# A conformer-pooling-SwiGLU block on eight cores: from four token tiles with a bf16 weight scratch to all 2048 tokens resident

## The reference

```python
u = rms_norm(h, g_mix); z = u @ w_in                      # (T, 5 x 1024)
gates = sigmoid(z[3072:] + b_gate)
a = z[:1024] * sigmoid(z[1024:2048])
a = depthwise_conv31(a) + b_dw
y_conv = silu(layer_norm(a, ln_g, ln_b)) @ w_conv_out
m = window_mean(z[2048:3072], (2, 4, 8, 16)) - z[2048:3072]   # 256 channels per window
y_pool = ((m @ w_pool) * pool_scale) @ w_pool_out             # w_pool: 4 blocks of 256 x 256
h = h + (gates[:1024] * y_conv + gates[1024:] * y_pool) @ w_o
v = rms_norm(h, g_ffn)
h = h + (silu(v @ w_ffn_gate) * (v @ w_ffn_up)) @ w_ffn_down  # 2816 wide
out = rms_norm(h, g_final)
```

## Time and profile before

| | |
|---|---|
| median of 3 runs | 1390.31 us (1389.91 to 1393.74) |
| span of the profiled execution, slowest core | 1385.0 us |
| spans of the 8 cores | 1373.7 to 1385.0 us |
| mean granted clock of PE, slowest core | 0.927 |
| busy: PE, DVE, ACT, POOL | 1115.2, 370.9, 339.1, 164.3 us |
| DMA | 229.35 MB, mean 166 GB/s |

### The profile page before, as it was taken

How to read it: one execution, slowest core, us unless ns; L and a number is a source line. 1 busy time by engine, 2 the same in 40 slices (tenths; PEclk the granted TensorE clock), 3 DMA queues, 4 the chain that set the end, 5 groups by cost and what they waited for, 6 DMA issues and landing times.

```text
span 1385.0 us, 16637 instructions; the slowest of 8 cores (1373.7 to 1385.0 us)
## 1 busy us (share of the span) xinstructions
PE 1115.2 (81%) x5862; PEld 505.4 (36%) x5960; DVE 370.9 (27%) x569; ACT 339.1 (24%) x519; POOL 164.3 (12%) x201
## 2 busy tenths in 40 slices
PE   0167587956656799879899998797999998898996
PEld 0033233332222344334444443244444443335443
DVE  0110432221111031532331314513221316323212
ACT  1112252122110023341331122522320234313111
POOL 6050202201000012011000102011000120110001
PEclk9988878987877899989999999899999999899999
DMA  9999999999999876525544457237424664253241
GB/s 165 185 211 192 221 159 168 184 177 173 173 171 157 194 240 150 174 96 170 190 153 168 155 176 208 91 122 246 165 108 173 217 196 139 104 188 148 97 162 61
DMA packets 85773, 229.35 MB, mean 166 GB/s; under 512 B 8351, under 2 KB 60191, under 8 KB 68925
## 3 DMA queue, kind: packets, MB, share of 16 engines
q1 hardware_dynamic: 42512, 166.30, 38.1%
q0 software_dynamic: 38528, 45.09, 24.5%
q10 hardware_dynamic: 4653, 16.90, 3.7%
HBM read 234.69 MB, written 45.09 MB: 202 GB/s over the span
## 4 chain that ended last, share of the span: by engine, by line
PE 46%; another core or an unknown queue 20%; DMA 11%; SPq 11%; DVE 5%; issue 4%; ACT 2%; POOL 1%; DVEq 0%; ACTq 0%; POOLq 0%
PE ps L431 43%; SPq L174 11%; DMA rep_59<-aT 3%; DMA wsc<-w_in 3%; PE ps L552 2%; DMA xres_100<-xe 2%; DMA xres_101<-xe 1%; DMA rep_58<-aT 1%; DVE rstd_ln L673 1%; DVE ub_62 L449 1%; DVE tn_80 L684 1%; PE ps L459 1%; DMA wslot_43<-wsc 0%; ACT sqj L437 0%
## 5 line engine op out<-in xcount | busy, mean ns | idle before, releaser
L441 POOL TENSOR_TENSOR stats<-stats,nhalf_s 128x1 f32<-128x1 f32 (+1 forms) x49 | 27.1, 554 | 634.0 <-DVE stats L439 634.0
L431 PE MATMUL ps<-vT,wslot_45 128*128 128x512 bf16 (+1 forms) x252 | 57.8, 375 | 33.5 <-DMA wslot_45<-wsc 13.2
L431 PE MATMUL ps<-vT,wslot_47 128*128 128x512 bf16 (+1 forms) x283 | 64.8, 373 | 16.9 <-DMA wslot_47<-wsc 10.5
L439 DVE TENSOR_SCALAR stats<-stats 128x1 f32<-128x1 f32 (+1 forms) x49 | 7.5, 153 | 201.3 <-ACT sqj L437 201.3
L431 PE MATMUL ps<-vT,wslot_46 128*128 128x512 bf16 (+1 forms) x267 | 58.0, 360 | 2.0 <-ACT vT L463 1.3
L431 PE MATMUL ps<-vT,wslot_43 128*128 128x512 bf16 x220 | 54.1, 386 | 6.4 <-DMA wslot_43<-wsc 5.4
L459 PE MATMUL ps<-ident_s,ub_61 128*128 128x128 bf16 (+1 forms) x136 | 10.9, 227 | 59.2 <-DVE ub_61 L449 34.6
L431 PE MATMUL ps<-vT,wslot_48 128*128 128x512 bf16 (+1 forms) x250 | 56.4, 365 | 0.9 <-ACT uT_49 L463 0.6
L431 PE MATMUL ps<-vT,wslot_44 128*128 128x512 bf16 (+1 forms) x236 | 54.9, 376 | 1.5 <-ACT vT L463 1.3
L836 DVE TENSOR_TENSOR fT<-ps,sgf_106 128x512 bf16<-128x512 f32 x44 | 30.4, 690 | 90.3 <-PE ps L431 84.4
L747 POOL TENSOR_TENSOR mergedT<-t_0_93,t_0_94 128x512 bf16<-128x512 f32 x16 | 20.2, 1264 | 287.5 <-DVE t_0_93 L744 287.5
(11 more groups left out here) (226 smaller groups left out, 1861.5 us busy)
## 6 DMA issues: line engine op xcount, KB each, us to landing
wslot_44<-wsc SPq DMA_DIRECT2D x22, 1024.0 KB, 9.3
wslot_47<-wsc SPq DMA_DIRECT2D x22, 1024.0 KB, 9.0
wslot_43<-wsc SPq DMA_DIRECT2D x21, 1024.0 KB, 10.6
wslot_45<-wsc SPq DMA_DIRECT2D x21, 1024.0 KB, 7.2
wslot_46<-wsc SPq DMA_DIRECT2D x21, 1024.0 KB, 8.2
wslot_48<-wsc SPq DMA_DIRECT2D x21, 1024.0 KB, 9.7
wsc<-w_in POOLq DMA_DIRECT2D x10, 1024.0 KB, 47.1
rep_58<-aT SPq DMA_DIRECT2D x96, 67.5 KB, 2.8
```

The costliest lines, as they stand in the source:

```text
L431: S.op(PE, lambda e: e.matmul(out, lhsT=lhsT, rhs=rhs, start=start, stop=stop), [lhsT, rhs], [out], signal=signal)
L441: S.op(POOL, lambda e: e.tensor_tensor(out=rs, in0=ms, in1=nhalf[0:n, 0:1], op=ALU.pow), [ms, nhalf[0:n, 0:1]], [rs])
```

## The change

The loop over tiles goes: all 2048 tokens of a core stay on chip, channel-major, and each step of the block runs over all of them.

- **Layout.** The host hands over x, the output and the weights already cut into channel-major blocks. x comes as 5 pieces of 416 tokens, halo included (`xp`), and once more as 4 blocks of 512 (`xr`) for the residual. PE transposes nothing. The RMS norm sums squares over channels: ACT squares, DVE adds the 8 channel groups, one fp32 matmul against ones (1/1024) adds the partitions, and ACT makes exp(-0.5 ln(.)).
- **Weights.** The scratch goes. POOL's DMA reads a chunk of 512 KiB in fp32 and casts it on the way into one of 9 slots, once per kernel (`load_one`); 108 such chunks and 8 of the FFN's down weights (1.4 MiB read each), which have places of their own. `w_pool` comes in fp32, uncast.
- **Order.** `pool_tile` for all pieces; then for each channel group `vg(c)`, `conv(c-1)`, `im2col(c)`; then LayerNorm statistics, fold, gates and projections, output projection, FFN, down projection in four blocks, the last in two halves.
- **im2col.** `a_out` writes a channel group to DRAM (`a_d`) in two parts, and eight DMAs read shifted copies back to `rep`.
- **LayerNorm statistics.** DVE adds d and its square over the channel groups (`acc_s`, `acc_q`); 8 fp32 matmuls instead of 64.
- **Pool map.** `w_pool` x `pool_scale` x `w_pool_out` is multiplied on chip to `weff` (32 matmuls of 512 columns), and the map's own matmuls per token go.
- **Background work.** Window sums and LayerNorm steps lie in a queue `bg` from which `pump(n)` emits n pieces between other instructions on DVE.
- **Spill.** After the output projection h1 is written to DRAM (`h1_d`) and read back for the last addition.

```diff
-        S.dma(SP, slot_sem[s], wslot[s][:, 0:nel], wsc.ap()[n][:, 0:nel], xr=[DRAM_G0 + n])
...
-            dsta = aT[:, :, 0:2 * HALO]
-            S.op(POOL, lambda e: e.tensor_copy(out=dsta, in_=acarry[:, :, 0:2 * HALO]), [acarry[:, :, 0:2 * HALO]], [dsta])
...
-        def im2col(pr):
-            for j in range(4):
-                for s_ in range(4):
-                    ws = 540 if s_ < 3 else 539
-                    o = repS[st][32 * s_:32 * s_ + 32, j, :, 0:ws]
-                    i_ = aT[32 * j:32 * j + 32, 2 * pr:2 * pr + 2, s_:s_ + ws]
-                    S.dma(SP, rep_sem[st], o, i_, val=tot)
...
-    for i in range(NT):
-        tile_body(i)
...
+NSLOT = 9
...
+    def load_one():
+        name, src, raw = wl[wnext[0]]
+        wnext[0] += 1
+        s = free.popleft()
+        whome[name] = s
+        dst = slotf[s][:] if raw else slot[s][:]
+        S.dma(POOL, slot_sem[s], dst, src)
...
+    x_load(0)
+    for _ in range(2):
+        load_one()
+    S.wait_prod(POOL, x_sem[0])
+    prefetch()
+    S.wait_prod(SP, slot_sem[3])
+    x_load(1)
+    S.wait_prod(SP, slot_sem[7])
+    x_load(2)
+    x_load(3)
...
+    def s1_rstd(p):
+        mm(psum[6][:, 0:PW], ones[:], sq0[p % 2][:, 0, :], True, True)
+        act(lnt[:, 0:PW], psum[6][:, 0:PW], AF.Ln, bias=e_rms)
+        act(psum[7][:, 0:PW], lnt[:, 0:PW], AF.Exp, scale=-0.5)
...
+    s1_squares(0)
+    s1_rstd(0)
+    s1_scale(0)
+    for p in range(NPC):
+        if p + 1 < NPC:
+            s1_squares(p + 1)
+        for c in range(KC):
+            pool_tile(p, c)
+            if c == 2 and p + 1 < NPC:
+                s1_rstd(p + 1)
+                s1_scale(p + 1)
+            if p == NPC - 1:
+                release(f"pool{c}")
+        if p == 0:
+            x_load(4)
...
+            while step < wd:
+                nw = width - step
+                dst = (s1, s2)[tgl][:, 0:nw]
+                out.append(lambda dst=dst, a=src[:, 0:nw], b=src[:, step:step + nw]:
+                           tt(DVE, dst, a, b, ALU.add))
+                src, width = dst, nw
+                step *= 2
+                tgl ^= 1
...
+    def vg(c):
+        for p in range(NPC):
+            sl = slice(p * PW, (p + 1) * PW)
+            bv, bg_ = nb(), nb()
+            for k in range(KC):
+                mm(bg_[:, 0:PW], w(f"gate{c}", k), uT[:, k, sl], k == 0, k == KC - 1)
+            for k in range(KC):
+                mm(bv[:, 0:PW], w(f"val{c}", k), uT[:, k, sl], k == 0, k == KC - 1)
+            s_ = sg[p % 2][:]
+            act(s_, bg_[:, 0:PW], AF.Sigmoid)
+            tt(DVE, aT[c % 2][:, sl], bv[:, 0:PW], s_, ALU.mult)
+            if p == 2:
+                a_out(c, 0, 3 * PW)
+            pump(2)
+        a_out(c, 3 * PW, EXT)
+        release(f"gate{c}", f"val{c}")
+    def a_out(c, lo, hi):
+        h = 0 if lo == 0 else 1
+        S.dma(SP, ad_sem[h], a_d.ap()[c][:, lo:hi], aT[c % 2][:, lo:hi], xw=[("ad", c, h)])
+    def im2col(c):
+        for h in range(2):
+            S.wait_prod(SP, ad_sem[h])
+            tot = rep_sem[h].count + 16 * 4
+            for s_ in range(4):
+                src = a_d.ap()[c].rearrange("(j i) t -> i j t", j=4)[:, :, HW_ * h + s_:HW_ * h + s_ + RW]
+                S.dma(SP, rep_sem[h], rep[h][32 * s_:32 * s_ + 32, :, 0:RW], src, val=tot)
+    def conv(c):
+        pump_until(win_done, c)
+        for b in range(NB):
+            h = b // 2
+            ps = nb()
...
+            if c == 1:
+                tt(DVE, acc_s[:, tok], d_sb[0][b][:], d_sb[1][b][:], ALU.add)
+            elif c > 1:
+                tt(DVE, acc_s[:, tok], acc_s[:, tok], d_sb[c][b][:], ALU.add)
+            if c > 0:
+                tt(DVE, acc_q[:, tok], acc_q[:, tok], dq, ALU.add)
+            pump(1)
+        if c + 2 < KC:
+            build_cw(c + 2)
...
+    vg(0)
+    im2col(0)
+    for c in range(1, KC):
+        vg(c)
+        conv(c - 1)
+        im2col(c)
...
+    def A(c, b):
+        ps = tile_mm(f"gA{c}", u_rhs(b))
+        i = sA[c, b] = ztile()
+        act(zt[i][:], ps[:], AF.Sigmoid, bias=pcc(PC_BGA, c))
...
+    def Bm(c, b):
+        ps = tile_mm(f"gB{c}", u_rhs(b))
+        i = t2[c, b] = ztile()
+        act(zt[i][:], ps[:], AF.Sigmoid, bias=pcc(PC_BGB, c))
+    def P(c, b):
+        ps = tile_mm(None, lambda k: mT[:, k, b * TT:(b + 1) * TT], weff_c=c)
+        i = t2[c, b]
+        tt(DVE, zt[i][:], ps[:], zt[i][:], ALU.mult)
...
+    def C(c, b):
+        pump_until(ln_done, b)
+        ps = tile_mm(f"co{c}", lambda k: actT[k][b][:])
+        i, j = sA.pop((c, b)), t2.pop((c, b))
+        tt(DVE, zt[i][:], ps[:], zt[i][:], ALU.mult)
+        tt(DVE, mrg[c][b][:], zt[i][:], zt[j][:], ALU.add)
...
+        mm(pm[:], ones[:], acc_s[:, tok], True, True)
+        mm(pq[:], ones[:], acc_q[:, tok], True, True)
+        i = ztile()
+        act(zt[i][:], pm[:], AF.Square)
+        if b == NB - 1:
+            mean, rstd = pm, psum[7]
+            ids = (i,)
+        else:
+            m_ = ztile()
+            act(zt[m_][:], pm[:], AF.Copy)
+            mean, rstd = zt[m_], zt[i]
+            ids = (i, m_)
+        tt(DVE, zt[i][:], pq[:], zt[i][:], ALU.subtract)
+        act(zt[i][:], zt[i][:], AF.Ln, bias=e_ln)
+        act(rstd[:], zt[i][:], AF.Exp, scale=-0.5)
+        lnm[b] = (mean, rstd, ids)
...
+                d = d_sb[c][b][:]
+                tt(DVE, d, d, mean[:], ALU.subtract)
+                tt(DVE, d, d, rstd[:], ALU.mult)
...
+            ts(DVE, wps[:, g, km, :], src, pcc(PC_PSC, 2 * g + km), ALU.mult)
+        for ki in range(2):
+            for h in range(2):
+                ps = nb()
+                for km in range(2):
+                    mm(ps[:], wps[:, g, km, ki * 128:(ki + 1) * 128],
+                       w(f"po{2 * g + km}", None, h * 512, (h + 1) * 512), km == 0, km == 1)
+                act(weff[:, 2 * g + ki, h * 512:(h + 1) * 512], ps[:], AF.Copy)
+            pump(1)
+        release(f"wpl{g}", f"po{2 * g}", f"po{2 * g + 1}")
...
+    for c in range(1, KC):
+        for b in range(NB):
+            A(c, b)
+            pump(1)
+            Bm(c, b)
+            pump(1)
+            P(c, b)
+            pump(1)
+        release(f"gA{c}", f"gB{c}")
+        for b in range(NB):
+            C(c - 1, b)
+        release(f"co{c - 1}")
...
+    def v_norm(b):
+        h = h1b[b % 3]
+        for c in range(KC):
+            stt(DVE, vT[:, c, b * TT:(b + 1) * TT], h[:, c, :], pcc(PC_GFFN, c), psum[7][:],
+                ALU.mult, ALU.mult)
+        S.dma(SP, sp_sem[b], h1_d.ap()[b], h[:].rearrange("p k t -> p (k t)"))
...
+    for j in range(2, NFC):
+        for b in range(NB):
+            gu(j, b)
+        release(f"fg{j}", f"fu{j}")
+        if j < 2 + KC:
+            c = j - 2
+            S.dma(POOL, fd_sem[c], wfd[c][:].rearrange("p j m -> p (j m)"), w_fd.ap()[c])
...
+    parts = [(0, 0, TT), (1, 0, TT), (2, 0, TT), (3, 0, 256), (3, 256, 256)]
+    for n, (b, o, w_) in enumerate(parts):
+        for c in range(KC):
+            ps = nb()
+            for j in range(NFC):
+                mm(ps[:, 0:w_], wfd[c][:, j, :], fT[j][:, b * TT + o:b * TT + o + w_], j == 0, j == NFC - 1)
```

1119 lines of the change are left out of this document (453 added, 666 removed).

## The result

The changed kernel took 1093.85 us in the median of its five runs beside 1390.31 for the kernel before, 296 us less. It was forecast at 1078, so the forecast was 1.4% short. Executions in which some cores ran at a lower granted clock than the rest (in one of these five 0.84 to 0.86 on one die, and 1231 us) are left out of the ratios and of the times in the experiments. The ratio is 0.785 (95% interval 0.781 to 0.789), from a median of 1091.39 us.

What follows compares the result with a forecast made beforehand. PE was taken as the bound: 985 us of its work plus 32, 5, 16, 12, 5, 6 and 11.5 of idle time and half clock made a 1072.5 us span, 1078 with 5.3 around it; range 1045 to 1165.

Steps and rivals of the forecast that it cites:

- idle in the value/gate loop: Value/gate loop: DVE, at 21.0 us a channel, nearly the bound for six channels; PE idle 5 us (0 to 15).
- start, up to the value/gate loop: Kernel start and pool phase: first matmul at 24 us, another wait of some 8; 32 us idle (24 to 45).
- LayerNorm and fold, idle: Between value/gate loop and gates: PE waits for ACT's four chains and the fold's scaling, 16 us (9 to 22).
- C(0, 3), idle: First convolution projection of block 3: its last 8 normalization steps come late on DVE, 12 us (5 to 14).
- seams of output projection and FFN: PE's idle time at the seams of the output projection and FFN, 5 us.
- the term for half clock: Whole kernel: PE at its lower clock level after four waits, 1.8 us each, 6 us.
- DMA: DMA keeps ahead of PE: 15.3 us a value/gate channel against PE's 21.4, trip covered, cost zero; share under 0.8.
- The first rival: Value/gate loop: a_d and rep move at 108 GB/s, 29.8 us a channel; time 1146; DMA-bound chance 0.21.
- The lower clock: All eight cores granted clock 0.80 under dense matmuls, adding 246 us: 1324; chance 0.08.
- Slower by weight latency: Value/gate, gates and FFN: weight chunks land too late; whole gain lost from 85 us, near 1880 at 126.7; chance 0.05.
- Ln and Exp: LayerNorm chains on ACT: if both share one table set, one load serves both and the sum is 7 us lower.
- Around the span: Time outside the slowest core's span, 5.3 us as in the kernel before, added at the end.

Runs made afterwards that it cites:

- The two experiments on the start: Changed kernel with ScalarE's squares issued a piece sooner, 1078.74 us; and, separately, with token piece 1 loaded right behind piece 0, 1083.17 us.
- the combined kernel: Changed kernel with squares sooner, piece 1 sooner, scalings spread, two LayerNorm steps a tile, weight scaling first, later Ln/Exp, fold copies shared with VectorE: 1057.82 us, ratio 0.755.

## Why the prediction was right, and where it was short

The mechanism held: the span is PE's work plus a few holes. Its terms, against core 3 of the changed kernel:

| term | predicted | measured |
|---|---|---|
| value/gate channel, PE | 21.4 | 21.2 |
| FFN and down with their sums, behind the first tile | 456.9 | 459.1 |
| idle in the value/gate loop | 5 | 1.1 |
| start, up to the value/gate loop | 90 | 112.1 |
| LayerNorm and fold, idle | 16 | 14.4 |
| C(0, 3), idle | 12 | 8.6 |
| seams of output projection and FFN | 5 | 12.5 |
| tail | 11.5 | 10.1 |

(456.9 is 304.1 less the first 16 matmuls, 152.4 and the fp32 sums, four of 0.86 and one of half the width; LayerNorm and fold 289.94 to 318.12 less 13.8 of matmuls; C(0, 3) is PE's waits for SiLU tiles; the seams are 73.8 less 61.3 of matmuls; the tail is 1079.7 to 1089.8.)

Taken together the idle terms came out (32 + 5 + 16 + 12 + 5 + 11.5 = 81.5 us priced, 80.0 measured), but by luck: the start and the seams were too short, the value/gate loop, the fold and C(0, 3) too long. The 17 us that are missing from the span are in the term for half clock. PE was busy for 1009.8 us where I had 985 and 6; summed from PE's timeline, the tiles behind its waits took some 22 us longer than the same tiles at full clock.

- **The start** is the step that failed, and with it the term for half clock. I priced the first matmul at 24 us (27.3) and one more wait of some 8 (6.55), and then let PE run: the prediction named a pool phase that ends far from 90 us as the sign of a mis-sized start, and it ended at 112.1. The missing 22 us are 3.3 at the first matmul, three waits of 2.64 that I had no term for, some 10 at half clock behind all these (my 6 us of half clock were for the whole kernel), and 3.1 of the pieces' sums, which I had counted with PE's work, less 1.5 at the wait for piece 1. What I overlooked is that ACT's squares of piece p+2 stand behind the last copy of piece p. The two experiments on the start take 12.6 and 8.1 us of it, together 18.
- **The seams** were priced at 5 without looking at what stands ahead of the additions on DVE. Spreading the scalings takes 11 of the 12.5 us.
- **DMA.** A value/gate channel was priced at 15.3 us; the share of 0.72 in the middle channels is 15.3 of 21.2. The sum is right, its parts are not: the cast landed 160 GB/s instead of 108, so the trip through DRAM took more than its 10.5. It stays covered, though the share was not under 0.8 everywhere (0.92 and 0.86 in the windows from 125 to 175 us); without cover it costs 15 us a channel. The first rival's time, near 1146, is passed when every im2col is read twice (1190), part of it by DMA time and part by the order in the queue.
- **The lower clock** did not come in the profiled run: 0.98 to 1.00 in every window in which PE is busy throughout, 0.973 to 0.978 over the spans of the eight cores. The Trainium skill (TensorE: Matmul & The Clock Gate, "Seeing it yourself") would have 13/16 under dense matmuls of several cores of a die; the profiled run disagrees.
- **Slower by weight latency**: weights landed in 4 to 5 us in the FFN, far from the 85 that decide, and a doubled load left them at 4.4 and 5.8.
- **Ln and Exp.** The Trainium skill (ScalarE: Activation LUTs, "Table sets: the hidden batching unit") has them in one set; the trace agrees, with one load of 1.28 us at 292.96 and the next at 319.03. The LayerNorm term still came out near 16 rather than near its low end of 9, and that is luck: its upper end had two table loads a chain, and one came for all four chains, but behind the 6.2 us for the scaling came 3.0 for two late weights, 1.0 for a copy and half clock, none of which I had priced there.
- **C(0, 3).** I counted 24 of 32 LayerNorm steps as done before the first reader comes; the fold pumps eight and not four, so that four steps were left and not eight. They stand on DVE behind the six operations of C(0, 0) to C(0, 2), and ACT's SiLU waits 4.07 us for the first.
- **Around the span** I added 5.3 us as before; the profiled execution took 1.6 (1091.39 for 1089.8).

Open: what makes the kernel before differ by 0.7% between the two comparisons (1390.31 and 1400.47 us) in which the changed one differs by less than 0.1% (1091.39 and 1091.82); how the gain divides between the scratch's first pass and the later waits; the last wait of the combined kernel; its gates beside the Ln and Exp moved there.

## What to carry to other kernels

When every long stage is bound by one engine, its work can be summed to within one per cent (here 21.4 for 21.2 and 456.9 for 459.1 us); the error sits at the seams, so write down for each seam what stands ahead of the awaited instruction on its own engine, and add the half clock behind each wait, here some 22 us in all. A block of work emitted in one piece (eight scalings, four chains, a piece's copies) delays everything behind it; spreading the scalings gained 13 us, while moving the sums behind them to a faster engine lost 12, since it put a wait for another engine at the head of that engine's queue. A DMA share under 1 is no licence to add transfers: add up their DMA time, and ask which later write will stand behind them in the same queue.

## What the runs showed of the hardware

- A DMA that casts fp32 to bf16 landed 160 GB/s (219 us of the sixteen engines for 35.13 MB), half as fast again as the 108 worked out from the kernel before.
- A write of 312 KB issued behind sixteen reads of 263 KB on one queue took 18.0 us to land instead of 2.2 to 2.6, at a DMA share of 0.76 to 0.95.
- Without three waits of PE of 2.64 us, 7.9 in all, the first convolution came 12.6 us sooner; half clock behind waits is most of the difference.
- The sum of two 128x512 fp32 tiles took 1.27 us on POOL and 0.69 on DVE, and yet the kernel was faster with it on POOL.
